# Softmax normalisation one slot later and the weight split one slot earlier in the attention slots of a hybrid decoder layer

## The reference

```python
s = einsum('bqhd,bkhd->bhqk', q[:, q0:kend], k[:, :kend]) * scale
s = where(mask, s + c[q] - c[k], -inf)      # c: running sum of log forget gates
p = softmax(s, axis=-1)
out = einsum('bhqk,bkhd->bqhd', p, v[:, :kend])
```

## Time and profile before

| | us |
|---|---|
| median of three runs | 1095.99 |
| lowest, highest | 1095.81, 1096.52 |
| the profiled execution's own time | 1095.99 |
| its span, first to last instruction | 1094.2 |
| PE busy | 1077.5 (98%) |
| DVE busy | 667.9 (61%) |
| ACT busy | 503.5 (46%) |

### The profile page before, as it was taken

One profiled execution on the slowest core, in us unless ns is written; L12 is line 12 of the kernel. 1 busy time (PEld: TensorE's weight loads), 2 busy tenths in 40 slices (PEclk: granted clock), 3 DMA queues, 4 the chain that ended last, 5 costly groups with the idle time before them and its releaser, 6 DMA issues.

```text
span 1094.2 us, 15984 instructions
## 1 busy us (share of the span) xinstructions
PE 1077.5 (98%) x6558; PEld 960.9 (88%) x6558; DVE 667.9 (61%) x809; ACT 503.5 (46%) x728; POOL 34.6 (3%) x76
## 2 busy tenths in 40 slices
PE   7999999999999999999999999999999999999997
PEld 5899999998888978888888888889899999988886
DVE  6788888873334663476655233458778787853334
ACT  7355455452223573667773222344454545442222
POOL 2000000000001100000000000011000000000001
PEclk9999999999999999999999999999999999999999
DMA  9622422434322544222114335315424234143311
GB/s 288 193 78 78 155 78 83 149 97 173 96 80 58 174 118 118 74 77 78 40 39 138 101 99 172 105 40 173 155 79 153 78 95 138 77 169 118 98 39 77
DMA packets 115203, 121.13 MB, mean 111 GB/s; under 512 B 6192, under 2 KB 100416, under 8 KB 115136
## 3 DMA queue, kind: packets, MB, share of 16 engines
q1 hardware_dynamic: 112960, 115.47, 34.0%
q10 hardware_dynamic: 1456, 2.10, 0.9%
q0 software_dynamic: 720, 2.62, 0.7%
HBM read 111.80 MB, written 6.29 MB: 108 GB/s over the span
## 4 chain that ended last, share of the span: by engine, by line
PE 87%; DVE 6%; ACT 2%; issue 2%; DMA 2%; POOL 1%; SPq 1%; ACTq 0%; DVEq 0%; POOLq 0%
PE bank L1395 25%; PE bank L1481 11%; PE bank L1483 11%; PE bank L1482 11%; PE bank L1385 6%; PE bank L1387 6%; PE bank L1386 6%; PE bank L1603 1%; PE bank L1604 1%; PE bank L1605 1%; DVE w_lo L901 1%; PE bank L1450 1%; PE bank L1451 1%; PE bank L1452 1%; DMA raw<-in_ffn_w_up 1%
## 5 line engine op out<-in xcount | busy, mean ns | idle before, releaser
L1481 PE MATMUL bank<-tc,w_hi 128*128 128x256 f32 x576 | 163.1, 283 | 0.3 <-ACT scr L606 0.3
L1482 PE MATMUL bank<-tc,w_hi 128*128 128x256 f32 x576 | 163.0, 283 | 0.0
L1483 PE MATMUL bank<-tc,w_lo 128*128 128x256 f32 x576 | 163.0, 283 | 0.0
L901 DVE TENSOR_TENSOR w_lo<-raw,w_hi 128x1024 fp32r<-128x1024 f32 x72 | 87.8, 1221 | 98.1 <-ACT w_hi L515 98.0
L1395 PE MATMUL bank<-w_hi,a_hi 128*128 128x512 f32 x408 | 126.1, 390 | 0.0
L1395 PE MATMUL bank<-w_hi,a_lo 128*128 128x512 f32 x408 | 125.6, 389 | 0.0
L1395 PE MATMUL bank<-w_lo,a_hi 128*128 128x512 f32 x408 | 125.6, 389 | 0.0
L1385 PE MATMUL bank<-u_hi,w_hi 128*128 128x512 f32 x312 | 123.6, 396 | 0.2 <-issue 0.2
L1481 PE MATMUL bank<-u_hi,w_hi 128*128 128x256 f32 x432 | 122.4, 283 | 1.3 <-DVE scr L1028 1.3
L1015 DVE TENSOR_TENSOR w_lo<-raw,w_hi 128x1024 fp32r<-128x1024 f32 x36 | 44.1, 1226 | 129.3 <-ACT w_hi L593 129.3
L1483 PE MATMUL bank<-u_hi,w_lo 128*128 128x256 f32 x432 | 122.3, 283 | 0.0
(11 more groups left out here) (235 smaller groups left out, 2068.7 us busy)
## 6 DMA issues: line engine op xcount, KB each, us to landing
raw<-in_w_in SPq DMA_DIRECT2D x40, 512.0 KB, 3.8
raw<-in_ffn_w_down SPq DMA_DIRECT2D x36, 512.0 KB, 3.5
raw<-in_ffn_w_gate SPq DMA_DIRECT2D x10, 1024.0 KB, 5.4
raw<-in_ffn_w_up SPq DMA_DIRECT2D x10, 1024.0 KB, 8.0
h<-in_ffn_w_gate SPq DMA_DIRECT2D x8, 1024.0 KB, 5.4
h<-in_ffn_w_up SPq DMA_DIRECT2D x8, 1024.0 KB, 8.3
raw<-in_ffn_w_up SPq DMA_DIRECT2D x8, 512.0 KB, 5.2
h<-in_x SPq DMA_DIRECT2D x8, 512.0 KB, 6.9
```

The source lines that it names most:

```text
L901: V.tensor_tensor(w_lo[:, slot(u), :], raw[:, slot(u), :], w_hi[:, slot(u), :].bitcast(F32), ALU.subtract).then_inc(lo_ready, 1)
L1481: mm(dst, w_hi[:, slot(u), w], moving(n, 0, k), start=first and k == 0, stop=False, skip_group_check=True)
L1482: mm(dst, w_hi[:, slot(u), w], moving(n, 1, k), start=False, stop=False, skip_group_check=True)
L1483: last = mm(dst, w_lo[:, slot(u), w], moving(n, 0, k), start=False, stop=k == KD // 2 - 1, skip_group_check=True)
```

## The change

N(s) and R(s) move from slot s to slot s+1: on DVE R(sl-1) comes right after M(sl), so DVE no longer waits for E(sl) there; on ACT N(sl-1) comes after E(sl) and the filler read, ahead of C(sl-2). `w_hi` on ACT moves ahead of the work of `gla_slots`, and so do the two key transfers of `spread_keys`. `w_lo` on DVE moves from the end of slot sl+1 into slot sl, behind `kin` (L1311) and ahead of the `o` operations. No instruction is added or taken away.

```diff
 # ACT, slot sl, behind E(sl) and the filler read
+                if 1 <= sl <= NS:
+                    s = sl - 1
+                    act.wait_ge(rinv_ready, s + 1)
+                    nc.scalar.activation(probs[steps[s][1]], probs[steps[s][1]], ACT.Copy,
+                                         scale=rinv[:, s:s + 1]).then_inc(probs_ready, 1)
                 if 2 <= sl < NS + 2:
                     s = sl - 2
                     act.wait_ge(pt_ready, s + 1)
...
                     nc.scalar.activation(ga, gb, ACT.Exp, scale=-1.0 / TAU).then_inc(a_act, 1)
+                if sl in FILLED:
+                    split(v + 4, second=(second_in[0], 32) if v + 4 == U_GATE + 2 else None)
+                if sl - 1 in FILLED and FILLERS[FILLED[sl - 1]][0] == "k":
+                    spread_keys(FILLERS[FILLED[sl - 1]][1])
                 for g in gla_slots.get(sl, ()):
...
-                if sl < NS:
-                    act.wait_ge(rinv_ready, sl + 1)
-                    nc.scalar.activation(probs[qb], probs[qb], ACT.Copy,
-                                         scale=rinv[:, sl:sl + 1]).then_inc(probs_ready, 1)
-                if sl in FILLED:
-                    split(v + 4, second=(second_in[0], 32) if v + 4 == U_GATE + 2 else None)
-                if sl - 1 in FILLED and FILLERS[FILLED[sl - 1]][0] == "k":
-                    spread_keys(FILLERS[FILLED[sl - 1]][1])
 # DVE, slot sl
-                if sl < NS:
-                    dve.wait_ge(exp_done, sl + 1)
-                    V.reciprocal(rinv[:, sl:sl + 1], rowsum[:, sl:sl + 1]).then_inc(rinv_ready, 1)
+                if 1 <= sl <= NS:
+                    s = sl - 1
+                    dve.wait_ge(exp_done, s + 1)
+                    V.reciprocal(rinv[:, s:s + 1], rowsum[:, s:s + 1]).then_inc(rinv_ready, 1)
...
                     V.tensor_tensor(kin, kin, ga, ALU.mult).then_inc(a_dve, 1)
+                if sl in FILLED:
+                    split(U_FILL + FILLED[sl] + 4)
                 if sl in gated_slots:
...
                         V.tensor_tensor(sq_lo, msq[:, n, :], sq_hi.bitcast(F32), ALU.subtract).then_inc(sq_lo_out, 1)
-                if sl - 1 in FILLED:
-                    split(U_FILL + FILLED[sl - 1] + 4)
```

## The result

The changed kernel takes 1104.72 us (median of four runs, 1103.09 to 1105.30) against 1095.95 us for the kernel before in the same runs: a ratio of 1.0078, 95% interval 1.0066 to 1.0090. It is slower by 8.8 us between the medians; 5.5 had been forecast, and the time lies 0.3 us above the range. The profiled execution took 1105.26 us, 9.3 more than before. All 31 executions of the changed kernel on record lie between 1103.03 and 1106.77 us, and the lower their mean granted clock, the longer they are: the four of 0.999 took 1103.0 to 1103.2 us, the thirteen of 0.997 took 1105.2 us or more, but for one of 1104.15.

The account below looks back on a forecast made before the run. PE was taken to bound the kernel, busy 1077.5 of 1094.2 us. Losses of 2.9 + 0.3 + 2.3 = 5.5 us on 1095.99 gave 1101.5 us, range 1097.3 to 1104.4.

Parts of the forecast that it names:

- R one slot later: DVE's 26.0 us of waiting go, but nothing on PE waited for it: 0 to 0.9 us gained, taken as 0.
- Slots 13 to 17: E(15), N(14) and the chain w_hi, w_lo, M(16) delay the second kst copy; PE loses 2.9 us, bounds 2.1 and 2.9.
- Slot 18: N(17) comes behind E(18) and the filler read, so T(17) begins 0.3 us late; bounds 0 and 0.8.
- Slots 25 to 32: T(25) 0.4 us late, M(27) +1.13, M(31) +2.33, so T(30) begins 2.35 us late; bounds 0.4 and 2.7.
- The clock: Rival: PE's pause in slot 17 brings back a slow clock, 2.3 us more, 1103.8; above 1103 0.09, shared with further waits.
- No change: Rival: DVE's removed waits bring maxima earlier, M(16) isn't held up, T(30) keeps its room: 1096.5 us; chance 0.18.
- faster: Rival: removed waits pull E and T forward and short hidden PE waits, about 3.2 us, return: 1092.8 us; chance 0.03.
- The signs: PE waits some 3 us at L1661, 2 at L1699; w_lo waits for w_hi; PE busy time unchanged; falling clock column refutes.

Follow-up runs that it names:

- e4_norm_only: Kernel before with only N and R one slot later, w_hi and w_lo left at the end of their slots: 1101.09 us.
- e13_weights_only: Changed kernel with N and R back in their own slots, so only the w_hi and w_lo moves remain: 1095.91 us.
- e3_pe_busy: Changed kernel plus ten unread 128x512 products on PE ahead of its wait for the second kst copy in slot 17: 1103.35 us.
- e10_norm_after_copy: Kernel before with N and R one slot later, but N(sl-1) behind C(sl-2) instead of ahead of it: 1100.73 us.
- e8_norm_first: Kernel before with N and R one slot later, but N(sl-1) right behind E(sl), ahead of the filler read: 1102.75 us.
- e6_wlo_only: Kernel before with only w_lo moved into its unit's slot; w_hi stays last on ACT, N in its slot: 1103.23 us.
- e1_lo_late: Changed kernel with w_lo of every filled slot put back to the end of the next slot on DVE: 1102.92 us.
- e9_pe_busy5: Changed kernel plus five unread 128x512 products on PE at the start of its wait in slot 17: 1102.84 us.
- e11_after_mended: Changed kernel with N(sl-1) behind C(sl-2) and w_lo at the end of the next slot; w_hi stays early: 1101.69 us.

## Why the prediction was right and wrong

- **R one slot later, worth 0.** Right. What I hadn't followed is where the wait goes: all 26 us turn up in L's wait for C.
- **Slots 13 to 17, 2.9 us.** The size was nearly right: the `attn` product is 3.24 + 0.28 = 3.5 us late, since E(15) came 0.5 us later than walked. The cause was wrongly divided. I gave N(14) 0.51, the serial chain of w_hi, w_lo and M 1.58, and the rest to slot 14 in the same way. e4_norm_only loses 1.58 us up to T(15) with no part of that chain; e13_weights_only has the whole chain and loses nothing. A walk of the sum of all edits gives the time of the sum, and says little of what each edit is worth.
- **Slot 18, 0.3 us.** In the changed kernel it isn't there: T(16) and T(17) are 6.17 and 6.18 late, because the slow clock holds PE back by more. With the clock up (e3_pe_busy, e4_norm_only) T(17) is 0.3 later than T(16), as walked.
- **Slots 25 to 32, 2.35 us.** Mis-sized: 9.29 - 6.14 = 3.15 from T(21) to T(31). T(25) 0.4 as walked. M(27) goes from 6.65 at M(26) to 7.79, 1.14 (walked 1.13). M(31) is 2.58 behind T(23) (walked 2.33). What was missing is the `attn` product of slot 25, 0.5 us, which waits for the mean square copy; I had left it 0.1 to 0.3 us of room and put it outside the sum.
- **The clock.** This is the step that failed: the sum put the price of a fallen clock at nothing. The rival was named, priced at 2.3 us and given less than 0.09, since the column in the earlier trace rows says 1.00 behind a wait of 7.6 us. That row was misread. The trace of the kernel before has no record of a granted clock ahead of 11.98 us, and where there is none the column shows 1.00. The products themselves tell more: they follow one another at 0.43 us before that time and at 0.23 after it (lines below this list). The runs show 2.9 us in the changed kernel (T(16) 6.17 late, the `attn` product 3.24) and 2.4 net. With its own price in the sum the forecast would have been 1103.8, 0.9 us below the measured median, and the range would have reached higher.
- **No change, and faster.** Neither came: no PE wait of the kernel before was removed.
- **The signs.** The waits at L1661 and L1699 and those of w_lo came as foretold (2.5 us, 2.8 us and 13 waits). Two didn't hold, PE's unchanged busy time (3.8 us more) and the clock column, whose fall had been named as a sign that the prediction is wrong.

PE at the start of the kernel before, two products per line:

```profile
8.65 1.06 PE L1559 MATMUL bank<-u_hi,w_lo 128*128 128x512 f32 x2
9.50 1.06 PE L1562 MATMUL bank<-u_lo,w_hi 128*128 128x512 f32 x2
...
15.63 0.62 PE L1553 MATMUL bank<-u_hi,w_hi 128*128 128x512 f32 x2
16.08 0.62 PE L1559 MATMUL bank<-u_hi,w_lo 128*128 128x512 f32 x2
```

The mechanism that the runs leave standing: M, E, filler read, C, L and the next M form a loop over ACT and DVE in each slot. In the kernel before N and w_hi stand behind C, while DVE does L and M, so they cost the loop little. One slot later N stands inside it or waits for the transposes, at each of the three places tried. The first T that comes over 0.5 us late is T(12) in e10_norm_after_copy, T(14) in e4_norm_only and T(15) in e8_norm_first, in slots 14 to 17; that DVE's long operations of slots 8, 12 and 14 have used up the room by then is my reading, and no run took them away. w_lo in its own slot is harmless while ACT does N beside it (e13_weights_only), and harmful when N isn't there or when w_hi is last (e6_wlo_only). N and R alone cost 4.4 us, the weight split 0; the remaining 9.6 - 4.4 = 5.2 us exist only when both are there: 2.0 with w_hi alone added (e1_lo_late), 3.2 more with w_lo, and 2.4 of them are the clock. That N's cost comes from the loop is shown only in part: the 43.2 us of L and the `kst` copy of e10_norm_after_copy speak for it, but putting N behind C didn't give the time back, and why T(8) and T(12) then run out of room was not taken further.

## What to carry to other kernels

When one engine is full, ask of each instruction on the others not when its result is needed but what it is beside: the normalisation was needed a slot later, and was free only because it ran while the other engine did its part of the loop. A wait that is removed from an engine inside such a loop reappears at the next hand-over; look for the other wait that grows by the same amount. And price a wait of the matrix engine of a few microseconds with the clock that may fall behind it: in the profiled execution here that was 2.4 us on top of 2.5. Read the speed at the pause from the spacing of equal products too, and not from a column alone.

## What was not expected of the hardware

How long PE stands still doesn't alone decide whether the clock falls, nor when. Behind waits of 2.45, 2.2 and 1.9 us in slot 17 it fell (changed kernel, e8_norm_first, e6_wlo_only), behind 1.3 and 0.9 us it didn't (e9_pe_busy5, e4_norm_only). In the changed kernel it fell during the wait, 0.45 us before its end; in the other two at 502.5 and 502.1, when PE had been at work again for 2.2 and 1.9 us. It stayed down for 6.8 us in the first and 3.4 in the others. And in e10_norm_after_copy it fell around a wait of 0.61 us, in slot 31. PE's timeline there, and the stretches of one microsecond, whose third column from the end is the clock:

```profile
553.53 1.77 PE L1686 MATMUL bank<-arena,scr 64*128 64x64 f32 x14
...
556.93 0.56 PE L1701 MATMUL bank<-ident,scr 128*128 128x128 f32 x2 [0.61 <-ACT scr L806]
557.15 2.59 PE L1711 MATMUL bank<-pt,og 128*128 128x512 f32 x8
...
556.00:557.00 1.00, 0.39 (x4) 0.13 (x3) 0.65 (x2) 1.00 (x4) 0.00 (x0) 1.00 0.00 0
557.00:558.00 1.00, 1.00 (x4) 0.90 (x5) 0.35 (x3) 0.97 (x3) 0.00 (x0) 0.55 0.00 0
558.00:559.00 1.00, 1.00 (x4) 0.90 (x4) 1.00 (x2) 1.00 (x2) 0.00 (x0) 0.50 0.00 0
```

The eight products that take 1.48 us at full clock take 2.59 here. Ahead of the wait stand fourteen products of 64x64, a transpose and a score row. The Trainium skill, "TensorE: Matmul & The Clock Gate", section "Part 4: PE-mode transpose", says that transposes don't count as activity in the way that other products do, and they stand on both sides of this pause. But neither they nor the small products decide it: e11_after_mended has the same instructions of PE in the same order at this place, with a wait of 0.62 us, and its clock stays at 1.00.

```profile
554.77 1.77 PE L1686 MATMUL bank<-arena,scr 64*128 64x64 f32 x14
...
558.18 0.44 PE L1701 MATMUL bank<-ident,scr 128*128 128x128 f32 x2 [0.62 <-ACT scr L806]
558.37 1.48 PE L1711 MATMUL bank<-pt,og 128*128 128x512 f32 x8
...
558.00:559.00 1.00, 0.82 (x5) 0.74 (x6) 0.48 (x2) 1.00 (x3) 0.00 (x0) 1.00 0.00 0
```

Waits of 0.5 us at T(29) didn't bring the clock down either (changed kernel, e4_norm_only), one of 0.79 did (e8_norm_first), one of 1.23 at T(30) of e11_after_mended didn't. The executions of one kernel differ too. A stretch of 3.4 us at half the clock takes the mean over the span to 0.998 or lower. Of the five executions of e10_norm_after_copy three have 0.999 or 1.000, so it isn't in them; two have 0.997, the profiled one among them. Of the changed kernel's 31, four have 0.999. All four of e11_after_mended and all four of e9_pe_busy5 have 0.999 or 1.000. So the same program loses to the clock in one execution and nothing in another. What tells them apart no run here shows.
